# Stick-breaking attention steps in a two-layer transformer kernel: the next logits in front of the projection's products on TensorE, and VectorE's rests one step later

## The reference, cut to what matters

```python
def stick_breaking_attention(q, k, v):
    for blk in range(s // SB_BLOCK):              # 8 blocks of 128 queries
        logits = jnp.einsum("bqhd,bkhd->bhqk", q[:, q_start:k_end], k[:, :k_end]).astype(jnp.float32) * scale
        strict = (q_start + jnp.arange(SB_BLOCK))[:, None] > jnp.arange(k_end)[None, :]
        log_beta = jax.nn.log_sigmoid(logits)
        log_keep = jnp.where(strict, jax.nn.log_sigmoid(-logits), 0.0)
        log_tail = lax.cumsum(log_keep, axis=3, reverse=True) - log_keep
        weights = jnp.where(strict, jnp.exp(log_beta + log_tail), 0.0).astype(v.dtype)
        outs.append(jnp.einsum("bhqk,bkhd->bqhd", weights, v[:, :k_end]))
```

## Time and profile before

| | us |
|---|---|
| median of 3 runs | 2663.93 |
| lowest and highest | 2662.77, 2664.5 |
| the profiled execution: its own time | 2653.37 |
| the profiled execution: its span | 2651.6 |
| the stage of the change in that span | about 1519 to 1856 |

### The profile page before, as it was taken

One profiled execution on the slowest core, in us unless ns is written; L12 is line 12 of the kernel. 1 busy time (PEld: TensorE's weight loads), 2 busy tenths in 40 slices (PEclk: granted clock), 3 DMA queues, 4 the chain that ended last, 5 costly groups with the idle time before them and its releaser, 6 DMA issues.

```text
span 2651.6 us, 32495 instructions
## 1 busy us (share of the span) xinstructions
PE 2557.0 (96%) x12496; PEld 2112.1 (80%) x12496; DVE 1529.8 (58%) x2345; ACT 789.4 (30%) x1353; POOL 188.4 (7%) x94
## 2 busy tenths in 40 slices
PE   7999999999999999998999999989999999999998
PEld 6777787888888888787888877777788888888886
DVE  6668265444344437646454577778566555646466
ACT  2245041111011102535433355544532121212122
POOL 6303300000000000001222200000000000000000
PEclk9996999999999999998999999979999999999999
DMA  3403613223232323113110001021012121202011
GB/s 121 37 9 81 79 33 93 93 77 94 86 93 77 94 86 117 31 42 116 32 42 27 25 17 33 17 96 38 19 56 64 33 63 32 63 32 63 32 56 72
DMA packets 201576, 157.05 MB, mean 59 GB/s; under 512 B 56184, under 2 KB 176512, under 8 KB 201472
## 3 DMA queue, kind: packets, MB, share of 16 engines
q1 hardware_dynamic: 183344, 124.94, 16.5%
q10 hardware_dynamic: 18128, 30.71, 4.4%
HBM read 147.23 MB, written 11.56 MB: 60 GB/s over the span
## 4 chain that ended last, share of the span: by engine, by line
PE 87%; DVE 6%; ACT 2%; issue 2%; DMA 2%; SPq 1%; POOL 1%; ACTq 0%; DVEq 0%; PEldq 0%; POOLq 0%
PE pd L818 25%; PE pd L820 25%; PE pd L819 25%; PE pt L1338 1%; PE pd L1385 1%; DMA raw<-in_w_out 1%; PE pd L1307 1%; PE pt L1400 1%; PE pt L818 1%; PE pt L1416 1%; PE pt L1355 1%; PE pt L838 1%; PE pt L1418 1%; PE pt L820 1%; PE pt L819 1%
## 5 line engine op out<-in xcount | busy, mean ns | idle before, releaser
L818 PE MATMUL pd<-actT_hi,st_hi 128*128 128x512 f32 x1872 | 749.3, 400 | 7.0 <-DVE st_lo L2233 3.6
L820 PE MATMUL pd<-actT_hi,st_lo 128*128 128x512 f32 x1872 | 733.4, 392 | 0.0
L819 PE MATMUL pd<-actT_lo,st_hi 128*128 128x512 f32 x1872 | 732.6, 391 | 0.0
L818 PEld LDWEIGHTS pd<-actT_hi,st_hi 128*128 128x128 f32 x1872 | 354.0, 189 | 76.9 <-ACT evac L1573 3.9
L820 PEld LDWEIGHTS pd<-actT_hi,st_lo 128*128 128x128 f32 x1872 | 353.2, 189 | 75.2
L819 PEld LDWEIGHTS pd<-actT_lo,st_hi 128*128 128x128 f32 x1872 | 354.4, 189 | 66.6
L818 PE MATMUL pd<-mv_hi,hid_hi 128*128 128x512 f32 x864 | 337.3, 390 | 3.5 <-DVE acc L2547 1.5
L819 PE MATMUL pd<-mv_lo,hid_hi 128*128 128x512 f32 x864 | 336.5, 389 | 0.0
L820 PE MATMUL pd<-mv_hi,hid_lo 128*128 128x512 f32 x864 | 336.3, 389 | 0.0
L1704 ACT ACTIVATE mv_hi<-raw 128x1024 fp32r<-128x1024 f32 x54 | 55.9, 1056 | 603.6 <-PE pd L820 478.1
L1573 ACT ACTIVATE evac<-pd 128x1024 f32<-128x1024 f32 x76 | 77.9, 1024 | 451.9 <-PE pd L820 451.9
(11 more groups left out here) (340 smaller groups left out, 3763.0 us busy)
## 6 DMA issues: line engine op xcount, KB each, us to landing
raw<-in_w_ff SPq DMA_DIRECT2D x64, 512.0 KB, 4.0
ada_raw<-in_w_ada ACTq DMA_DIRECT2D x64, 384.0 KB, 3.2
raw<-in_w_up SPq DMA_DIRECT2D x44, 512.0 KB, 3.8
raw<-in_w_in SPq DMA_DIRECT2D x30, 512.0 KB, 3.7
raw<-in_w_down SPq DMA_DIRECT2D x22, 512.0 KB, 3.4
acc<-in_x SPq DMA_DIRECT2D x16, 512.0 KB, 8.8
raw<-in_w_out SPq DMA_DIRECT2D x12, 512.0 KB, 3.4
raw<-in_w_ple_gate SPq DMA_DIRECT2D x8, 512.0 KB, 3.8
```

The lines of the kernel that those rows point to most:

```text
L818: pe.matmul(out_ap, a_hi, b_hi, start=start, stop=False, skip_group_check=check)
L819: pe.matmul(out_ap, a_hi, b_lo, start=False, stop=False, skip_group_check=check)
L820: return pe.matmul(out_ap, a_lo, b_hi, start=False, stop=stop, skip_group_check=check)
```

## The change

On TensorE, `scores3(s+1)` moves in front of `jobs3(s)` and `beside3(s)` in the odd turns. On VectorE, the rests of query and key results, and the rests of projection weights, are taken one turn later (from `stick_ends(s-2)`); the rest of a value transpose stays where it was. No instruction is added or taken away; ScalarE's, GpSimd's and SyncE's orders stay as they were.

```diff
@@ TensorE, the loop over s @@
                 if s >= 4:
                     outputs3(s - 4)
+                if s % 2 and s + 1 < NS:
+                    scores3(s + 1)
                 jobs3(s)
                 beside3(s)
-                if s % 2 and s + 1 < NS:
-                    scores3(s + 1)
@@ VectorE, the loop over s @@
                 if 1 <= s <= 3 * NB + 2:
-                    for q, e, kind, half in stick_ends(s - 1):
-                        job_lo(0, 4 * NJ1 + NJ2 * q, att2[q % 2], [(e, kind, half)], q)
+                    for q, e, kind, half in stick_ends(s - 1) + stick_ends(s - 2):
+                        if (kind == "T") == ((q, e, kind, half) in stick_ends(s - 1)):
+                            job_lo(0, 4 * NJ1 + NJ2 * q, att2[q % 2], [(e, kind, half)], q)
                 beside3(s)
...
                 if 1 <= s <= 3 * NB + 2:
-                    for q, e, kind, half in stick_ends(s - 1):
+                    for q, e, kind, half in stick_ends(s - 2):
                         if kind != "T" and half:
                             stick_weight_lo(next_unit(q, e))
```

## The result

| | before | after |
|---|---|---|
| median of 14 runs each, same chip, us | 2664.2 | 2642.92 |
| lowest and highest, us | 2648.33, 2672.55 | 2627.63, 2654.69 |
| ratio of the times | | 0.9916, 95% interval 0.9899 to 0.9933 |
| the profiled execution, us | 2653.37 | 2636.38 |

The changed kernel is faster by 0.84% by the ratio, which is 17.8 to 26.9 us by its interval; the medians are 21.3 us apart. A second comparison gave 0.9924 (0.9894 to 0.9954). The prediction was 2652.5 with a range down to 2645.5: the direction was right, but the gain is nearly twice the 11.4 us forecast, and the median lies outside the range.

The account below looks back on a forecast made before the run. TensorE, busy 96% of the span, was taken as the bound, leaving its idle and half-clock time. 6.4 + 1.3 - 1.3 + 4.1 + 0.3 + 0.6 = 11.4 us gained, so 2652.5 us; 8-in-10 range 2645.5 to 2660.

Parts of the forecast that it names:

- The stalls in the projection turns: Turns with projection work: VectorE's later rests remove TensorE's stalls of 2.85, 2.61, 0.36 and 0.6 us, 6.4 us gained.
- The clock behind the 2.85 us stall: From 1575 to 1577 us: about 2.7 us run at half clock, so without the stall 1.3 us more gained.
- The early logits in these turns: Projection turns: TensorE waits for ScalarE some 0.5 and 0.8 us in turns 5 and 9, 1.3 us lost.
- new neighbours: TensorE's changed order in 36 projection rounds: switches between kinds of work cost up to 3.6 us either way, taken as 0.
- ScalarE's path of "5.0 us": Heavy projection round: ScalarE's work between logits takes 5.0 us, even with TensorE's 5.0; other rounds have 0.3 us or more.
- The mixing transposes: Turns 75 to 78: logits fill TensorE's wait, so the first product of `first_half_row` starts 4.1 us sooner.
- nothing changes: Turns 78 to 94, the row products: TensorE is never idle there, so no gain.
- rival (a): Mixing turns: full clock returns earlier, a further 2 us and 2.5 more; total gain 13 to 18 us; chance 0.14.
- the 0.3 us of `v2b`: Turn 72: value hi part no longer stands behind late logits, 0.3 us off the 1.91 us stall; the rest stays.
- The last turns: End of the stage: VectorE's `w_lo` starts about 0.6 us earlier and the 3.03 us stall shrinks by 0.6 us.
- Rival (d): Projection stalls stay because VectorE's own work fills the round; only mixing turns gain 4 to 5 us; 0.22 shared with (b).
- Rivals (b) and (c): ScalarE delays TensorE's products: 7 us lost in 18 rounds, about 2660 (0.22 with (d)); or 18 us in 36, 2670 (0.07).

## Why the prediction was right in direction and too small

**The stalls in the projection turns: right, but read too low.** Predicted 6.4 us. TensorE's idle time between its matmuls there fell from 6.99 to 0.65 us, 6.3 us (one of the three stalls of 0.87 us stood in turn 10 of the first pair, at 1546.21 us, and not in a later pair). But the turns gained more than their rows of stalls show. The piece at `rows` is one of the two that were put at 0.6 us in all:

```profile
1608.08 0.33 PE L1416 MATMUL pt<-v2b,wt_hi 128*128 128x128 f32 x1 [0.31 <-DVE rows L2535]
```

From one set of transposes to the next, that turn of the kernel before is 0.62 us longer than the same turn after, twice the 0.31 in the row, because the weight load of the same product waited first, 0.55 us, and the matmul's row counts only what was left. Three more stalls of this kind show on the weight load alone; the matmul's own row lists no idle time:

```profile
1555.71 0.19 PEld L1416 LDWEIGHTS pt<-v2a,wt_hi 128*128 128x128 f32 x1 [0.45 <-DVE rows L2535]
```

The five together, in the weight loads' waits of the kernel before from 1518 to 1862 us:

```profile
PEld pt L1416 <- DVE rows L2535: 2.5, 5, 0.6
```

Each of these three turns is 0.33 us shorter after. The two kinds come to 2 x 0.31 + 3 x 0.33 = 1.6 us that the sum left out, since only the matmuls' waits were read.

**The clock behind the 2.85 us stall: right, a little small.** Predicted 1.3 us. The three turns around the stall are 4.57 us shorter after. Of this 2.85 is the stall, 1.7 the clock: it was at half for 3.4 us, in which the work of 1.7 us at full clock is done. The 2.7 us of the prediction were read too short. In the profile after, the clock at that place is full. The turns that had the stall, after the change:

```profile
1566.46 0.60 ACT L1609 ACTIVATE k_hi2b<-pd 128x512 fp32r<-128x512 f32 x1 [0.47 <-PE pd L820]
...
1567.88 1.28 DVE L2452 TENSOR_TENSOR_SCAN tail<-keep,tail 128x512 f32<-128x512 f32 x1
...
1570.14 0.68 DVE L2097 TENSOR_TENSOR k_lo2b<-pd,k_hi2b 128x512 fp32r<-128x512 f32 x1
...
1570.74 1.21 DVE L2080 TENSOR_TENSOR st_lo<-raw,st_hi 128x1024 fp32r<-128x1024 f32 x1
...
1572.09 0.60 PE L1400 MATMUL pt<-ident,stick 128*128 128x128 f32 x4
```

The scan now comes ahead of the rest and the weight rest, the hi part has long been there (written from 1566.46, read at 1570.14), and the transposes at 1572.09 wait for nothing. That is the step "the rest finds its hi part ready", as put.

**The early logits in these turns: the cost sized too high, and the sum wrong in sign.** Predicted a loss of 1.3 us in turns 5 and 9, and 0 from new neighbours. The waits are in the two turns named, but small. The matmuls' rows show one of them, in turn 9:

```profile
1546.82 0.33 PE L1385 MATMUL pd<-k_hi2a,q_hi2a 64*128 64x128 f32 x2 [0.19 <-ACT stick L1877]
```

In turn 5 only the weight load's row shows a wait, 0.25 us. From mark to mark the two cost more than the 0.19 us: turn 5 takes 3.28 us, against 3.09 in the kernel before, and turn 9 takes 3.35, against 3.09 for the same turn of the two later pairs. That is 0.4 to 0.5 us in all, where 1.3 had been forecast.

The step that failed is ScalarE's path of "5.0 us", which added up the durations in the rows. ScalarE's instructions overlap. The kernel before, ScalarE from 1540 us:

```profile
1539.76 0.60 ACT L1874 ACTIVATE keep<-pd 128x512 f32<-128x512 f32 x1 [1.59 <-PE pd L1391]
1540.25 0.59 ACT L1877 ACTIVATE stick<-pd 128x512 f32<-128x512 f32 x1
1540.72 0.60 ACT L1607 ACTIVATE q_hi2b<-pd 128x512 fp32r<-128x512 f32 x1
1541.20 1.08 ACT L1592 ACTIVATE st_hi<-raw 128x1024 fp32r<-128x1024 f32 x1
```

Their starts are 0.47 to 0.49 us apart, though each takes 0.60; the 1024-wide one takes 1.08 and the next starts 0.95 behind it. The path is about 0.1 us shorter for each instruction on it. In the profile after, the logits start 0.05 us after the end of the second sigmoid in turns 5 and 9, where TensorE waited for it, and 0.41 us after it in turns 33 and 57, the end of the round that was counted as even; so that round had some 0.36 us in hand. The two experiments with longer sigmoid work put a price on it: 0.5 us more in a turn costs 1.7 us in all, 1.0 us more costs 13.5.

And the neighbours are not 0. The rounds of two turns between turns 12 and 72 that have no stall, compared between the kernel before and the one with the early logits only, are 0.05 us shorter with them on average (the single rounds from 0.02 longer to 0.09 shorter); over 36 rounds that makes some 1.7 us. It lies within the 3.6 us that the prediction allowed. It agrees roughly with the rest of the account: 6.3 + 1.6 + 1.7 leaves 1.5 of the 11.1 us for the early logits with their cost in turns 5 and 9; and the changed kernel's projection turns are 1.8 us shorter than those of the kernel with late rests alone. It is seen where one kind of work follows another: transposes right behind logits took 0.65 us in the kernel before at 1586.97 us, and behind the products they take 0.60 after. Why a switch costs what it does was not tested and stays open.

**The mixing transposes: right but too small; and then the row products, which were put at nothing.** This is the step by which the forecast missed its range. The forecast was 4.1 us in this stretch, the measurement 5.4; and the row products, for which the prediction said that "nothing changes" in the turns 78 to 94, gave 2.7. Together that is 8.1 us; rival (a), with 4.1 + 2 + 2.5 = 8.6, had described it. The order is as laid out: the logits at 1741.88 start ahead of the second pair of transposes at 1743.63, and `keep` waits 1.11 us, not 3.82:

```profile
1741.88 0.69 PE L1385 MATMUL pd<-k_hi2b,q_hi2b 64*128 64x384 f32 x2
...
1743.63 1.93 PE L1429 MATMUL pd<-ident,rows 128*128 128x128 f32 x8
1743.65 0.49 ACT L1874 ACTIVATE keep<-pd 128x384 f32<-128x384 f32 x1 [1.11 <-PE pd L1391]
...
1745.37 0.69 DVE L2479 TENSOR_TENSOR actT_lo<-pd,actT_hi 128x512 fp32r<-128x512 f32 x1 [0.40 <-ACT actT_hi L1894]
...
1746.12 1.97 PE L1429 MATMUL pd<-ident,rows 128*128 128x128 f32 x8
```

VectorE's wait of 2.87 us is 0.40, and the stalls of 0.74 and 1.25 us are gone. The stretches of the same profile show the clock (the last is the start of the row products):

```profile
1744.00:1748.00 4.00, 4.00 (x21) 3.86 (x20) 3.40 (x7) 3.36 (x8) 0.00 (x0) 0.50 0.96 379
1748.00:1750.00 2.00, 2.00 (x15) 1.54 (x14) 1.97 (x5) 1.15 (x3) 0.00 (x0) 0.92 1.03 424
...
1753.00:1755.00 2.00, 1.52 (x7) 1.30 (x8) 1.97 (x3) 0.28 (x1) 0.00 (x0) 1.00 1.03 414
```

Half clock lasts 10.2 us around the transposes, against 27.3 us before, which reached far into the row products (0.50 at 1751 to 1759 and still 0.66 at 1771 to 1773). The Trainium skill, TensorE: Matmul & The Clock Gate, Part 1, says that the default is throttled and that activity releases it. The trace agrees only in part: TensorE has no idle row from 1738.23 on, yet its clock stays at half for some 10 us, and is 0.92 at 1748 to 1750. So a stretch without stalls came before the return, but what brought it back at 1748 the rows don't show.

The profiles of the other kernels bear on it. In us, from the first mixing transpose to the last turns (the kernels with longer sigmoids or moved weights left out):

| kernel | at half clock | mixing transposes | row products |
|---|---|---|---|
| before | 26.2 | 20.69 | 71.44 |
| before, again | 22.6 | 20.70 | 71.34 |
| late rests only | 17.1 | 19.74 | 71.53 |
| changed | 10.1 | 15.25 | 68.75 |
| changed, again | 13.0 | 15.26 | 70.38 |
| early logits only | 6.8 | 15.10 | 68.80 |
| early logits from turn 74 | 12.5 | 15.27 | 70.30 |

With the logits late the half clock lasts longer, in all three profiles, and 5.3 to 5.7 us of it lie in the row products, against 0 to 3.4 with the logits early. Half of 5.5 us is the 2.7 us gained there: that part of (a) is shown. In the mixing transposes themselves the clock counts for little. The kernel before takes 20.7 us with 20.7 or with 17.3 us of them at half, and the early logits 15.3 or 15.1 with 10.1 or 6.8. Of the 1.3 us that came beyond the 4.1, some 0.4 came in the first round, all at half clock: the next transposes start 7.9 us behind the first, where 8.3 had been laid out. So that the rest was the clock's, as (a) says, is argued and not shown.

The prediction gave (a) only 0.14. It read the long half clock as a state of the stretch, and took the duration at 1.2 GHz for all of it, up to and through the start of the row products; the profiles show that it shrinks with the order that removes the stalls. TensorE does wait again at full clock, as (a) said, 1.79 us at the first row product:

```profile
1738.23 1.97 PE L1429 MATMUL pd<-ident,rows 128*128 128x128 f32 x8 [1.91 <-DVE v2b L2100]
...
1753.48 0.47 PE L818 MATMUL pd<-w_hi,actT_hi 128*128 128x512 f32 x1 [1.79 <-DVE actT_lo L2479]
```

The first row is the stall that was to stay but for 0.3 us; it is 1.91 as before, so the 0.3 us of `v2b` can't be seen.

The clock behind the second row varies with the execution: full in this profile, where the row products take 68.75 us; half for 3.4 us in the second profile, 70.38; half for 5.5 us at the start of the row products in the kernel before, 71.44. So 1.1 to 2.7 us of the gain depend on it.

**The last turns: right.** Predicted 0.6, measured 0.6. The stall of 3.03 us is 2.42:

```profile
1826.80 1.05 PE L1400 MATMUL pt<-ident,stick 128*128 128x128 f32 x4 [2.42 <-DVE wt_lo L2461]
```

**The signs named in advance.** No wait of VectorE for `q_hi` and `k_hi`, no 2.85 us stall, no 0.87: all so. Stalls at line 1385 in turns 5 and 9: so, but small, and of the matmuls' rows only that of turn 9 shows one, 0.19 us. Logits ahead of the second pair of transposes: so. The first row product was to come about 4 us sooner behind the first transpose: it came 5.4 sooner. Rival (d), that VectorE's own work fills the round, is out: the stalls are gone with all of that work kept. Rivals (b) and (c) are out at this length of ScalarE's path and true at 1 us a turn more.

The steps that failed are thus three: the half clock, taken to be the same after the change, with the row products at nothing (3.7 us missed with the mixing turns); ScalarE's path, added up from durations, with the neighbours at 0 (2.8 us); and the stalls read from the matmuls' rows alone (1.5 us). Set beside the terms: 6.3 + 1.6 for stalls (predicted 6.4), 1.7 for the clock behind the long one (1.3), about 1.5 for the logits and their neighbours (-1.3), 5.4 and 2.7 in the mixing turns and behind them (4.1 + 0.3, and 0), 0.6 at the end (0.6). The differences from the prediction are 1.5, 0.4, 2.8, 3.7 and 0, that is 8.4 us, which with its 11.4 gives 19.8 of the 19.9 measured.

## What to carry over

Before you call an engine's path even, add up its start-to-start times, not the durations of its rows: on ScalarE this made a loss of 0.5 us look like one of 1.3. Read the weight load's waits beside the matmuls', and compare the same turn in both kernels from mark to mark, since a stall's row may show half of it. And where a stretch with stalls runs at half clock, work the sum out at both levels: removing the stalls can bring back the clock in what follows too. Here the larger sum was the nearer one.

## What the runs showed of the hardware that I had not expected

- A stall of 2.85 us was followed by half clock for 3.4 us in one execution of the kernel before and for 6.8 us in another. Shorter stalls can do it too: one of 1.88 us in the kernel with the early logits only was followed by 3.4 us, and a stall of 1.79 us at the first row product was followed by 3.4 us at half clock in the second profile of the changed kernel and by none in the first.
- Executions of identical code differ ahead of the stage: its first logits start between 1518.90 and 1536.39 us in the profiles, while what follows the stage takes 794.8 to 796.0 us in all eleven profiles. The 17 us ahead of it are more than the changes of clock in the stage come to (1.6 to 2.8 us in a stretch), so most of the scatter between runs of one kernel seems to come from ahead of it; its cause stays open. A single profiled execution says little about a median.
- ScalarE started a 512-wide activation 0.47 to 0.49 us behind the last one, while each row shows 0.60 us; a 1024-wide one held it for 0.95, not 1.08.
